# Halves-first start of the first projection, and another order of the last four tiles, in a three-block layer stack

## What is computed

```python
# first layer, first operation
u = x @ w_in + b_in                 # 1024 x 1024 by 1024 x 5632
c = glu_a * sigmoid(glu_b)          # two 512-wide parts of u
c = causal_depthwise_conv(c, conv_w, conv_b)      # width 31
# last layer, last operations
gate = sigmoid(rmsnorm(h, ple_norm_w) @ w_ple_gate)
h = h + (p @ w_ple_proj) * gate
return rmsnorm(h, final_norm_w)     # rows of 1024
```

## Time and profile before

| | us |
|---|---|
| median of three runs | 3282.16 |
| lowest and highest run | 3276.44, 3284.37 |
| the profiled execution | 3279.56 |
| its span, first to last instruction | 3277.7 |
| PE busy in the span | 3116.9 |
| mean granted clock, share of full | 0.981 |

### The profile page before, as it was taken

The page is one execution under the profiler, slowest core; times in us unless marked ns, Lnnn a source line. Parts: engine busy times, 40 slices in busy tenths (PEclk is TensorE's granted clock), DMA queues, the critical chain, the costliest instruction groups (busy, mean ns, idle before and its releaser), DMA issues.

```text
span 3277.7 us, 38033 instructions
## 1 busy us (share of the span) xinstructions
PE 3116.9 (95%) x15348; PEld 2444.3 (75%) x15348; DVE 1689.8 (52%) x2730; ACT 1129.9 (34%) x1910; POOL 955.3 (29%) x699
## 2 busy tenths in 40 slices
PE   8999989999989999999999978899999899999998
PEld 6776667666878888777887755687777688788876
DVE  6979651112546644243333467667667745543435
ACT  2125543112441121113331275444445422322334
POOL 4211001112417784125421112321011123442522
PEclk9999989999999999999999989999999999999999
DMA  4110001112312332114331101331011145433322
GB/s 125 51 32 20 14 14 45 39 52 109 130 58 82 90 115 76 45 48 145 112 94 33 39 27 52 116 98 33 26 46 46 36 125 125 133 135 109 103 71 102
DMA packets 251055, 242.22 MB, mean 74 GB/s; under 512 B 15360, under 2 KB 198016, under 8 KB 249856
## 3 DMA queue, kind: packets, MB, share of 16 engines
q1 hardware_dynamic: 228944, 195.52, 19.5%
q10 hardware_dynamic: 21936, 44.27, 3.9%
HBM read 201.03 MB, written 38.73 MB: 73 GB/s over the span
## 4 chain that ended last, share of the span: by engine, by line
PE 80%; DVE 8%; ACT 5%; DMA 2%; POOL 2%; issue 2%; SPq 1%; ACTq 0%; DVEq 0%
PE psum L539 21%; PE psum L541 21%; PE psum L540 21%; PE psum L657 3%; PE psum L545 3%; DMA arena<-in_w_in 2%; DVE arena L2792 1%; PE psum L703 1%; PE psum L729 1%; PE psum L1159 1%; PE psum L840 1%; PE psum L1110 1%; POOL WS L3070 1%; PE psum L1109 1%; DVE arena L2673 1%
## 5 line engine op out<-in xcount | busy, mean ns | idle before, releaser
L3070 POOL TENSOR_TENSOR WS<-arena,WS 128x1024 fp32r<-128x1024 f32 x271 | 673.8, 2492 | 1862.6 <-ACT WS L1175 1862.4
L539 PE MATMUL psum<-XH,WS 128*128 128x512 f32 x2464 | 986.4, 400 | 34.2 <-POOL XL L3126 15.6
L541 PE MATMUL psum<-XH,WS 128*128 128x512 f32 x2464 | 963.1, 391 | 0.0
L540 PE MATMUL psum<-XL,WS 128*128 128x512 f32 x2464 | 962.8, 391 | 0.0
L539 PEld LDWEIGHTS psum<-XH,WS 128*128 128x128 f32 x2464 | 464.6, 189 | 149.7 <-issue 30.1
L541 PEld LDWEIGHTS psum<-XH,WS 128*128 128x128 f32 x2464 | 464.5, 188 | 99.0
L540 PEld LDWEIGHTS psum<-XL,WS 128*128 128x128 f32 x2464 | 465.0, 189 | 96.3 <-issue 4.8
L1175 ACT ACTIVATE WS<-arena 128x1024 fp32r<-128x1024 f32 x271 | 284.7, 1059 | 677.5 <-PE psum L541 243.2
L539 PE MATMUL psum<-WS,XH 128*128 128x512 f32 (+1 forms) x1024 | 396.0, 387 | 19.4 <-DVE XL L2108 7.2
L540 PE MATMUL psum<-WS,XH 128*128 128x512 f32 (+1 forms) x1024 | 392.9, 384 | 0.0
L541 PE MATMUL psum<-WS,XL 128*128 128x512 f32 (+1 forms) x1024 | 392.5, 383 | 0.0
(11 more groups left out here) (291 smaller groups left out, 3257.9 us busy)
## 6 DMA issues: line engine op xcount, KB each, us to landing
arena<-in_w_in SPq DMA_DIRECT2D x85, 512.0 KB, 3.7
arena<-in_w_out SPq DMA_DIRECT2D x48, 512.0 KB, 3.3
arena<-in_w_in_even SPq DMA_DIRECT2D x48, 512.0 KB, 4.1
arena<-in_w_out_even SPq DMA_DIRECT2D x32, 512.0 KB, 3.2
h_spill<-arena ACTq DMA_DIRECT2D x24, 512.0 KB, 3.1
arena<-s_table SPq DMA_DIRECT2D x8, 1536.0 KB, 6.8
arena<-in_w_in_odd SPq DMA_DIRECT2D x18, 512.0 KB, 3.7
s_table<-arena SPq DMA_DIRECT2D x32, 256.0 KB, 3.0
```

The lines of the kernel that those rows point to most:

```text
L539: e.matmul(ps, wh, xh, start=start, stop=False)
L540: e.matmul(ps, wh, xl, start=False, stop=False)
L541: return e.matmul(ps, wl, xh, start=False, stop=stop)
L3070: e.tensor_tensor(lo, raw(book.raw_of.get(("w", u), 0), kbs, n), hi.bitcast(F32), SUB).then_inc(*w.up("w_lo", u))
```

## The change

At the start: x is asked for by halves. ACT issues the even `kb` of half 0 before anything else, then `cols`; SP issues weight block 0, the odd `kb` of half 0, weight block 1, all eight `kb` of half 1, and then the other constants and the row. ACT makes hi of block 0, copies half 0, makes hi of block 1, copies half 1. The lo parts of x are all made by DVE; POOL makes only those of the weights. The first two weight blocks (`glu_b` and `glu_a` of m = 0) go through `proj_first`: both on half 0, then both on half 1. `proj_first` takes the number of blocks from its argument. The event "fix" now stands for `cols` alone, PE doesn't wait for it at the start, and the other constants belong to "b1_cst", which was waited for already.

At the end: the sigmoid of the next tile is put between a tile's square and its root on ACT, DVE has the matching order, and the last tile's multiplication and store are done in two halves.

```diff
 (tensor) proj_first
-                for n in range(8):
-                    half, i = n // 4, n % 4
+                for n in range(2 * len(us)):
+                    half, i = n // len(us), n % len(us)
...
             ws.pump(2)
-            w.wait_ge("fix")
-            for m in range(4):
+            proj_first([((f"glu_{ab}", 0, 0), w_in[:, c:c + 128], lambda half, done=done: [(done, 0, half)])
+                        for ab, c, done in (("b", 2560, "glu_sig"), ("a", 2048, "glu"))], "b1", None, None)
+            for m in range(1, 4):
                 run(proj_cm("glu_b", (m,), ...
                 run(proj_cm("glu_a", (m,), ...
 (scalar) start
-            e.dma_start(cols, ap["cols"]).then_inc(*w.landed("fix", 0))
-            e.dma_start(ident, cst_in("ident")).then_inc(*w.landed("fix", 1))
-            e.dma_start(ones, cst_in("ones")).then_inc(*w.landed("fix"))
-            e.dma_start(m01, cst_in("m01")).then_inc(*w.landed("b1_cst", 0))
-            e.dma_start(mneg, cst_in("mneg")).then_inc(*w.landed("b1_cst", 1))
-            e.dma_start(vb1, row_in("v1")).then_inc(*w.landed("b1_cst"))
-            ws.pump(2)
+            for kb in range(0, 8, 2):
+                e.dma_start(XSTAGE[:, kb, half_of(0)], ap["xT"][tile_of(kb), half_of(0)]).then_inc(*w.landed(f"x_in{kb}_0"))
+            e.dma_start(cols, ap["cols"]).then_inc(*w.landed("fix"))
             for half in range(2):
-                for kb in range(0, 8, 2):
-                    e.dma_start(XSTAGE[:, kb, half_of(half)], ap["xT"][tile_of(kb), half_of(half)]).then_inc(
-                        *w.landed(f"x_in{kb}_{half}"))
-            for half in range(2):
+                ws.pump(half + 1)
                 for kb in range(8):
                     w.wait_ge(f"x_in{kb}_{half}")
                     e.activation(XH[:, kb, half_of(half)], XSTAGE[:, kb, half_of(half)], ACT.Copy).then_inc(
                         *w.up("x_hi", "b1", kb, half))
             w.wait_ge("fix")
-            for m in range(4):
...
+            run(proj_first([lambda half: glu_sig(0, half), lambda half: None], None, None))
+            for m in range(1, 4):
+                run(proj_cm(1, lambda _, half: glu_sig(m, half)))
                 run(proj_cm(1))
 (scalar) end; rms is split into Square and rms_root
-            for k in range(4):
-                g_ev(12 + k)
+            g_ev(12)
+            for k in range(3):
                 fin(4 + k)
+                g_ev(13 + k)
+                fin_root(4 + k)
+            fin(7)
+            fin_root(7)
 (vector) start
-                for kb in range(1, 8, 2):
+                for kb in range(8):
                     w.wait_ge("x_hi", "b1", kb, half)
 (vector) end; fin(tile, parts=1) multiplies in `parts` pieces
-            for k in range(4):
-                h4(12 + k)
+            h4(12)
+            for k in range(3):
+                h4(13 + k)
                 fin(4 + k)
+            fin(7, 2)
 (gpsimd) start
-            for half in range(2):
-                for kb in range(0, 8, 2):
-                    w.wait_ge("x_hi", "b1", kb, half)
-                    sl = half_of(half)
-                    e.tensor_tensor(XL[:, kb, sl], XSTAGE[:, kb, sl], XH[:, kb, sl].bitcast(F32), SUB).then_inc(
-                        *w.up("x_lo_p", "b1", kb, half, also=[("x", "b1", kb, half)]))
-            run(proj_cm(12))
+            proj_first(2)
+            run(proj_cm(10))
 (sync) start
-            ws.pump(2)
             for half in range(2):
-                for kb in range(1, 8, 2):
-                    e.dma_start(XSTAGE[:, kb, half_of(half)], ap["xT"][tile_of(kb), half_of(half)]).then_inc(
-                        *w.landed(f"x_in{kb}_{half}"))
-            run(proj_cm(12))
+                ws.pump(half + 1)
+                for kb in range(8):
+                    if half or kb % 2:
+                        e.dma_start(XSTAGE[:, kb, half_of(half)], ap["xT"][tile_of(kb), half_of(half)]).then_inc(
+                            *w.landed(f"x_in{kb}_{half}"))
+            for i, (dst, name) in enumerate(((ident, "ident"), (ones, "ones"), (m01, "m01"), (mneg, "mneg"))):
+                e.dma_start(dst, cst_in(name)).then_inc(*w.landed("b1_cst", i))
+            e.dma_start(vb1, row_in("v1")).then_inc(*w.landed("b1_cst"))
+            proj_first(2)
+            run(proj_cm(10))
 (sync) end
-            for tile in range(8):
+            for tile in range(7):
                 w.wait_ge("fin", tile)
                 e.dma_start(out[tile_of(tile), :], H3[:, tile, :]).then_inc(*w.landed("out", tile))
-            w.wait_ge("out", 7)
+            for half in range(2):
+                w.wait_ge("fin", 7, half)
+                e.dma_start(out[tile_of(7), half_of(half)], H3[:, 7, half_of(half)]).then_inc(*w.landed("out", 7, half))
+            w.wait_ge("out", 7, 1)
```

More of the change, by code:

```diff
@@ L1214, in proj_first @@
                     ws.load()
-                for n in range(8):
+                for n in range(2 * len(evacs)):
                     if n == at:
                         turn()
-                    if n >= 4:
+                    if n >= len(evacs):
                         ws.free()
-                    evacs[n % 4](n // 4)
+                    evacs[n % len(evacs)](n // len(evacs))
                     yield
@@ L1279, in load_h, with rms_root @@
                             *w.landed(f"h_in{i}", stage, also=[("h_in", stage, 2 * i), ("h_in", stage, 2 * i + 1)]))
+            def rms_root(stage, tile, r):
+                w.wait_ge("nrm_ms", stage, tile)
+                e.activation(r, r, ACT.Sqrt).then_inc(*w.up("nrm_rt", stage, tile))
             def rms(stage, tile, src, scr, r):
                 e.activation(scr, src, ACT.Square, accum_out=r).then_inc(*w.up("nrm_sq", stage, tile))
-                w.wait_ge("nrm_ms", stage, tile)
-                e.activation(r, r, ACT.Sqrt).then_inc(*w.up("nrm_rt", stage, tile))
+                rms_root(stage, tile, r)
             def norm_to_x(stage, H, gcol, scr_at, ready, free, x_free, spill=True):
@@ L1326, in scalar_program, with glu_sig @@
             w.wait_ge("fix")
-            for m in range(4):
[L1328 to L1332, removed]
+            def glu_sig(m, half):
+                w.wait_ge("glu_b", m, 0, half)
+                e.activation(C5[:, m + 1, 30 + 512 * half:542 + 512 * half], ps_of("glu_b", m, 0, half), ACT.Sigmoid,
+                             bias=col("b_in", 20 + m)).then_inc(*w.up("glu_sig", m, half))
+            run(proj_first([lambda half: glu_sig(0, half), lambda half: None], None, None))
+            for m in range(1, 4):
+                run(proj_cm(1, lambda _, half: glu_sig(m, half)))
                 run(proj_cm(1))
@@ L2056, in fin, with fin_root @@
                     w.wait_ge("nrm_rc", "fin", tile - 2)
-                rms("fin", tile, H3[:, tile, :], SQ3[tile % 2], small[:, 32 + tile:33 + tile])
+                e.activation(SQ3[tile % 2], H3[:, tile, :], ACT.Square, accum_out=small[:, 32 + tile:33 + tile]).then_inc(
+                    *w.up("nrm_sq", "fin", tile))
+            def fin_root(tile):
+                rms_root("fin", tile, small[:, 32 + tile:33 + tile])
             def g_evs(first, n):
@@ L2067, in scalar_program @@
                 fin(tile)
+                fin_root(tile)
             weave((proj_tm(512, tiles=range(4, 8)), 1, True), (g_evs(8, 4), 1, True))
-            for k in range(4):
-                g_ev(12 + k)
+            g_ev(12)
+            for k in range(3):
                 fin(4 + k)
+                g_ev(13 + k)
+                fin_root(4 + k)
+            fin(7)
+            fin_root(7)
         def vector_program(e, w):
@@ L3045, in h4, with fin @@
                 e.tensor_tensor(o, o, sg, A_).then_inc(*w.up("h4", ch, tile))
-            def fin(tile):
-                r, hx = small[:, 32 + tile:33 + tile], H3[:, tile, :]
+            def fin(tile, parts=1):
+                r, step = small[:, 32 + tile:33 + tile], 1024 // parts
                 rms("fin", tile, r, 1e-6)
@@ L3051, in fin @@
                 w.own()
-                e.scalar_tensor_tensor(hx, hx, r, G3, M, M).then_inc(*w.up("fin", tile))
+                for i in range(parts):
+                    sl = slice(step * i, step * i + step)
+                    hx = H3[:, tile, sl]
+                    e.scalar_tensor_tensor(hx, hx, r, G3[:, sl], M, M).then_inc(
+                        *w.up("fin", tile, i, also=[("fin", tile)] if i == parts - 1 else []))
             for n in range(8):
@@ L3100, in proj_th, with proj_first @@
                     yield
-            def proj_first():
-                for _ in range(4):
+            def proj_first(n=4):
+                for _ in range(n):
                     ws.load()
-                for _ in range(4):
+                for _ in range(n):
                     ws.free()
```

## The result

| | before | changed |
|---|---|---|
| median of the paired runs | 3282.94 us (3276.44 to 3289.22, 12 runs) | 3275.24 us (3270.36 to 3280.43, 12 runs) |
| profiled execution, its span | 3279.56, 3277.7 | 3279.37, 3277.2 |
| mean granted clock in it | 0.981 | 0.978 |
| first matmul | 15.62 us | 10.32 us |
| first four groups done | 39.82 | 34.46 |

The ratio of the times is 0.9975 [0.9967, 0.9982], a gain of 8.2 us [5.9, 10.8]. (A gain in this text is the median of before times one less the ratio; the two medians alone are 7.7 apart.) That is 0.25%, within the 0.3% that I had called indistinguishable; I forecast 12.2 us and 3268.4, and 3275.24 lies 0.2 above the upper end of the range.

What follows compares the result with a forecast made beforehand. PE, busy 3116.9 of 3277.7 us, was taken as the bound, so only the two ends could shorten: 6.8 (start) plus 5.4 (end) is 12.2 us, from 3280.6 to 3268.4, range 3262 to 3275.

Steps and rivals of the forecast that it cites:

- The end: After PE's last matmul: reordered ACT work saves 5.1 us, the halved last store 0.3, together 5.4 us.
- The start: Up to the fourth matmul group: done at 33.0 us against 39.82, a saving of 6.8 us.
- Step 1: Start: weight block 0, still SP's first request, lands after 4.4 us at 5.14; hi from 5.19, lo done at 8.65.
- Rival B: Start: x packets on ACT's queue delay weight block 0 to about 7.1, PE starts at 11.2; 10.2 us in all; chance 0.15.
- Step 4: First matmul group: 7.13 us as before; x and weight block 1 arrive barely in time, 0.3 us allowed for stalls.
- Rival E: First four groups: PE stays at the 0.43 us spacing, 88 matmuls cost 17.9 us, ending 5.7 slower, 3286.3; chance 0.03.
- Step 3: Start: DVE's first XL waits for POOL's lo and ends at 9.2; PE starts at 9.25, not 15.62, 6.4 us earlier.
- step 6: Second matmul group: it loses its stalls, 6.17 to 5.45 us, a saving of 0.7 us.
- The base: Starting time for the forecast: 3280.6 us, the mean of the profiled execution and three runs.
- C: PE's first groups: POOL and DVE obstruct each other, two more blocks of 2.4 us; total gain 7.4, 3273.2; chance 0.09.

Runs made afterwards that it cites:

- start only: Changed kernel with the old kernel's end put back, against the kernel before: 3281.07 against 3284.22 us, ratio 0.9989 [0.9980, 0.9998].
- x apart from w0: Changed kernel with ACT asking only for x block 0 and the columns, SP for x blocks 1 to 7 of half 0; first matmul 10.23 us, not timed.
- end only: Old kernel with only the change's new end, against the kernel before: 3278.11 us, ratio 0.9981 [0.9972, 0.9989].
- the repeat: The unaltered changed kernel timed once more against the kernel before: 3273.66 against 3282.90 us, ratio 0.9968 [0.9956, 0.9980].
- the two with the early stall: Changed kernel with weight block 0 in halves, lo by DVE, x copied first; the second also has weight block 1 halved behind half 0: ratios 0.9964, 0.9965.

## Why the prediction came out as it did

**The end** was right. Forecast 5.4 us, measured 5.7: the order of the work 5.25, the halves 0.42. Each of its steps stands in the rows of ACT above: sigmoid straight behind PE, a table load that runs ahead of the mean, and a table that stays for the last square and root. DVE's mean standing behind the next tile's products cost nothing, as said. What still stands in the way at the very end is the finishing product of tile 6 (DVE, 3271.47 to 3272.75): the mean of tile 7 starts behind it, and ACT's last root waits 0.58 us for it, where it waits 0.25 in the tiles before. The 2.15 us from square to product, taken from tile 3, came out at 2.14 (3271.15 to 3273.29).

**The start** had the right mechanism and two terms of the wrong size. 6.8 us forecast. The four groups are done at 34.4 to 34.6 in the four traces of the changed kernel's start with the new end, 5.2 to 5.4 before the first trace of before, and at 35.4 in start only, 4.5 before it. Over all five and the three traces with the old start (39.8 to 40.3) the means are 5.4 apart. The steps that failed:

- Step 1, "beside x blocks I take the same", 4.4 us to the landing of weight block 0. It took 5.4 (5.3 to 5.7 in the nine traces). First matmul at 10.32 and not 9.25: of the 1.07, 0.95 is this step (hi began at 6.14, not 5.19), and 0.1 is the wait behind POOL, PE 0.70 behind the end of lo in place of 0.60. Rival B had a later weight block at 2 us and 0.15; half of that came, and the three further x blocks that it blamed beside x block 0 made no difference in the run with x apart from w0.
- Step 4, "7.13 as before, slow start included", and 0.3 for stalls. The first group took 7.82 (18.14 - 10.32), with no stall in it; so 0.4 over the 7.43 of both. It has 11 matmuls at the spacing of 0.43, where the first trace of before has 7. But the second trace of before has 12 and took 8.04, start only has 14 and took 8.40, and end only, with the old start, took 7.24. So 7.13 was the smallest of a scatter of 1.3 us, and I had taken it as fixed because one trace was all there was. That it was the smallest is bad luck; that I gave it no width is the mistake.
- Rival E put the slow clock in as all or nothing, from 60 matmuls on. That was never near; in small it is in every version, with 7 to 17 slow matmuls, and with a gap early in the row it takes back part of what an earlier start gives.

Two steps were right. Step 3, POOL's lock: XL takes 2.44 us beside lo and 0.69 without, and copying x first took 0.41 us off the first matmul. The Trainium skill (SBUF — State Buffer, "Who interferes with whom") gives the exclusion as a rule. The two runs agree. And step 6: 5.44 us each for groups two to four.

**The sum.** 12.2 forecast, 11.0 in the ends of the traces: 1.5 for the two terms of the start, less 0.3 won at the end. The measured 8.2 and 10.5 have intervals of 5 and 8 us in width; the wider one holds 11.0 and the other misses it by a hair (10.8). Between 11.0 and the first comparison's 8.2 lie chance and, probably, a term that the sum put at nothing: "from there on PE, DVE's convolution and the weight stream stand to each other as before". The middles less their clock time bear that out within half a microsecond, but it says nothing of the granted clock. The twelve runs of the changed kernel lost 66.0 us to it on average, the runs with the old start 63.5. **The base** failed too: I took 3280.6 us, and the median of before is 3282.9 to 3285.1 in the larger comparisons. The execution I had summed against, 3279.56, ran at 0.981 and was one of the fastest. So of the 6.8 us between 3268.4 and 3275.24, 2.3 are the base, 1.2 the terms, and 3.3 clock and scatter. I had allowed 3 us beyond the rivals, and my own sum gives C's 3273.2 + 3 = 3276.2 for the upper end; the 3275 that I stated was narrower than that. **The chances**: 0.71 on a gain over 0.3%. A gain of 8 to 11 us lies across the 9.8 us of that bound. The forecast cleared it by 2.4 us, and with both terms as measured it clears it by 1.2, which is less than what the clock can take back. So 0.71 was too sure, and the 0.27 on a gain within 0.3% is what the first comparison shows (0.25%); the repeat shows 0.32%.

## What to carry to other kernels

Where an engine that is 95% busy sits between two short ends, price the ends from the traces and compare the ends, not the spans: the middle's clock varies by more than the gain from one execution to the next, and a single trace of each kernel invites a story about it. Where every run has its mean granted clock on record, average it over the runs of both kernels: that tells a loss of 2 us which no single comparison here can show. Before bringing a start forward, look when the next operands come: with three matmuls ahead of a stall, 0.4 and 1.6 of the 3.6 us by which PE began earlier were kept, since the matmuls behind the gap were still at the slow level (and in the first of the two PE waited for weight block 1 as well). At a tail in which ACT alternates two tables, put the next tile's work between square and root: the load then runs while another engine makes the mean.

## What the runs showed that I had not expected

- The lower level of TensorE's clock came and went in the middle of a kernel whose PE is 95% busy, 116 to 136 us in all of an execution, at mostly but not wholly the same places. The same window of the program reads 0.66 and 1.00 in traces of the changed kernel, and 1.00 and 0.67 in traces of before. It makes 3.3 us for 0.001 of mean clock, and a spread of 10 us among runs of one kernel.
- The places where it fell are ones at which PE has waits (the windows at 150 and at 400 us); from 3000 to 3100 us PE was busy throughout, and its clock read 1.00 in both first traces. Waits at a place don't suffice, though: the timed repeat of the changed kernel has them at 150 us and reads 1.00. That is as far as the rows go.
- At the start the slow level lasted 3.5 to 6.1 us in kernels whose first matmuls had no gap (before 15.62 to 19.07, start only 10.64 to 16.75), and 7.7 and 8.4 us in the two with the early stall. In the first group of those without one that makes a scatter of 1.3 us, which no edit explains.
- A first weight request of 512 KB lands in 4.4 to 5.7 us, its first half alone in 4.1 and 4.3; x block 0, 256 KB on the other queue, in 2.9 to 4.4.
- A product of DVE on one tensor and a number, f32 of 1024 elements, takes 0.69 us, and 2.43 or 2.73 when it meets a difference on POOL (2.35, 2.40), which it outlasts by 0.55.
